# State space projection in another unit order, with the early ada units over fewer steps and a ring of six

## The reference

```python
mod = c_act @ ada_w[i] + ada_b[i]                 # 2048 x 12288, one row vector
sh1, sc1, g1, sh2, sc2, g2 = split(mod, 6)
h = x * (1.0 + sc1) + sh1
u = h @ in_w                                      # 256 x 2048 by 2048 x 2048
lam_bar = exp(lam * dt)
b_bar = ((lam_bar - 1.0) / lam)[..., None] * bmat
bu = einsum('gnp,blgp->lbgn', b_bar, ug)
states = associative_scan(a * s + bu)             # over the tokens, complex
y = real(einsum('gpn,lbgn->blgp', cmat, states)) + d_skip * u
```

## Time and profile before

| | us |
|---|---|
| median of three runs (lowest, highest) | 2490.12 (2487.67, 2490.86) |
| the profiled execution, own time | 2485.89 |
| its span, first to last instruction | 2484.2 |
| TensorE, VectorE, ScalarE busy | 2394.9, 1853.9, 1045.8 |
| state recurrence, from and to | about 218 to 345 |

### The profile page before, as it was taken

The page is one execution under the profiler, slowest core; times in us unless marked ns, Lnnn a source line. Parts: engine busy times, 40 slices in busy tenths (PEclk is TensorE's granted clock), DMA queues, the critical chain, the costliest instruction groups (busy, mean ns, idle before and its releaser), DMA issues.

```text
span 2484.2 us, 33024 instructions
## 1 busy us (share of the span) xinstructions
PE 2394.9 (96%) x12457; PEld 1924.3 (77%) x12457; DVE 1853.9 (75%) x2964; ACT 1045.8 (42%) x1242; POOL 35.3 (1%) x67
## 2 busy tenths in 40 slices
PE   5799799999999999999999999999999999999998
PEld 3377468878888888888878888778888888888886
DVE  6377979977778887889878987887777755455457
ACT  4254024464443444344464444464544344434442
POOL 0000000000000000000000000000000000000000
PEclk9899899999999999999999999999999999999999
DMA  9996938858888998899758877736788666656674
GB/s 308 361 334 229 393 114 291 300 186 295 301 276 300 345 319 271 276 331 313 250 164 301 280 252 231 223 102 195 229 299 294 229 193 188 189 188 199 188 219 144
DMA packets 314686, 627.36 MB, mean 253 GB/s; under 512 B 30656, under 2 KB 31072, under 8 KB 314272
## 3 DMA queue, kind: packets, MB, share of 16 engines
q1 hardware_dynamic: 310240, 611.35, 73.5%
q0 software_dynamic: 4288, 13.90, 2.0%
HBM read 623.05 MB, written 2.10 MB: 252 GB/s over the span
## 4 chain that ended last, share of the span: by engine, by line
PE 85%; DVE 9%; DMA 3%; ACT 2%; issue 1%; SPq 0%; DVEq 0%; ACTq 0%
PE psB L2112 40%; PE psA L2112 39%; DVE prod L1424 2%; DMA col_raw<-in_ada_w 1%; PE psT L1707 1%; DVE tmp L1429 1%; DVE st L1435 1%; PE psM L1739 1%; PE psA L1947 1%; DVE w_lo L1103 1%; DMA Cnat_im<-in_s_c_im 0%; DMA w_raw<-in_dsa_out_w 0%; DVE ada_acc L1120 0%; DVE w_lo_more L1103 0%; DMA w_raw<-in_s_glu_w 0%
## 5 line engine op out<-in xcount | busy, mean ns | idle before, releaser
L1103 DVE TENSOR_TENSOR w_lo<-w_raw,w_hi 128x1024 fp32r<-128x1024 f32 x732 | 893.0, 1223 | 487.0 <-ACT w_hi L784 482.6
L784 ACT ACTIVATE w_hi<-w_raw 128x1024 fp32r<-128x1024 f32 x732 | 774.8, 1060 | 1110.0 <-PE psB L2112 483.6
L2112 PE MATMUL psB<-w_hi,hT_hi 128*128 128x512 f32 x1040 | 407.0, 391 | 0.6 <-DVE w_lo L1103 0.6
L2112 PE MATMUL psB<-w_hi,hT_lo 128*128 128x512 f32 x1040 | 404.9, 389 | 0.0
L2112 PE MATMUL psB<-w_lo,hT_hi 128*128 128x512 f32 x1040 | 404.7, 389 | 0.0
L2112 PE MATMUL psA<-w_hi,hT_hi 128*128 128x512 f32 x1008 | 397.9, 395 | 5.1 <-DVE w_lo L1103 2.0
L2112 PE MATMUL psA<-w_hi,hT_lo 128*128 128x512 f32 x1008 | 393.2, 390 | 0.0
L2112 PE MATMUL psA<-w_lo,hT_hi 128*128 128x512 f32 x1008 | 392.9, 390 | 0.0
L1120 DVE SCALAR_TENSOR_TENSOR ada_acc<-ada_raw,csil,ada_acc 128x512 f32<-128x512 f32 x450 | 336.1, 747 | 13.2 <-DVE ada_acc L1120 0.5
L2112 PEld LDWEIGHTS psB<-w_hi,hT_hi 128*128 128x128 f32 x1040 | 195.2, 188 | 44.7 <-issue 2.8
L2112 PEld LDWEIGHTS psA<-w_hi,hT_hi 128*128 128x128 f32 x1008 | 189.6, 188 | 49.5 <-issue 8.0
(11 more groups left out here) (368 smaller groups left out, 2330.0 us busy)
## 6 DMA issues: line engine op xcount, KB each, us to landing
w_raw<-in_ffn_w_in SPq DMA_DIRECT2D x352, 512.0 KB, 4.6
ada_raw<-in_ada_w SPq DMA_DIRECT2D x480, 256.0 KB, 5.4
w_raw<-in_ffn_w_out SPq DMA_DIRECT2D x176, 512.0 KB, 4.5
col_raw<-in_ada_w SPq DMA_DIRECT2D x128, 512.0 KB, 6.2
w_raw<-in_dsa_in_w SPq DMA_DIRECT2D x112, 512.0 KB, 4.8
w_raw<-in_s_glu_w SPq DMA_DIRECT2D x56, 512.0 KB, 5.7
w_raw<-in_s_in_w SPq DMA_DIRECT2D x32, 512.0 KB, 6.7
w_raw<-in_dsa_out_w SPq DMA_DIRECT2D x32, 512.0 KB, 5.4
```

The source lines that it names most:

```text
L784: nc.scalar.activation(high(u), w_raw[:, u % RING], ACT.Copy).then_inc(w_hi_ready, 1)
L1103: V.tensor_tensor(low(u), w_raw[:, u % RING], high(u).bitcast(F32), ALU.subtract).then_inc(w_lo_ready, 1)
L2112: ins = MM(PS[s][:, t, 0:r.width], a_[:, kt, tok], b_[:, kk, 0:r.width], start=kt == 0 and m == 0, stop=k == r.units - 1 and kk == UK - 1 ...
```

## The change

- `placed` replaces `crossed` and orders all 32 products: first k = 0 to 3 of i = 1, then k = 0 to 3 of i = 0, then k = 4 to 7 of i = 0, and k = 4 to 7 of i = 1 last.
- The half sums of i = 1 are copied from PSUM to `partial` by ScalarE after products 5 and 7; VectorE adds them when i = 1 ends (`finish`), where ScalarE had copied.
- `MIXED` is 40, and 24 columns stand beside products, two for each of twelve.
- The early ada units run from step 16 on (12 steps), in a ring of 6 slots (growA and part of uT, since `partial` has the region more). Slot 4 lies over the staging of h, so unit 4 waits for the last fourth of h (`h_ready`).
- The C table is scaled before BLdiag; `in_pair` and its columns stand before BLdiag is turned.
- `skip_diagonals` is cut in two: 8 tiles at step 30, 8 after the last uT.

```diff
-MIXED = FRONT - AU
+MIXED = FRONT - 24
...
-        early_raw = [at("early_raw0", "growA", [P, 4, AW]), at("early_raw1", "more", [P, 4, AW])]
+        early_raw = [at("early_raw0", "growA", [P, 4, AW]), at("early_raw1", "uT", [P, 2, AW], plus=8 * K)]
+        partial = at("partial", "more", [P, 2, TOK, NB])
...
-        s5_in = Run("u", 2, s5_in_w[0], (0, NB), dense=(0, EARLY, 4, 10), before="x")
+        s5_in = Run("u", 2, s5_in_w[0], (0, NB), dense=(0, EARLY, 4, 16), before="x")
...
-        beside = (4, 4, 4, 2, 2, 0, 0, 0)
-        crossed = [(k, s) for k in range(6) for s in range(2)] + [(6, 0), (7, 0), (6, 1), (7, 1)]
+        beside = (0, 2, 2, 2, 2, 2, 2, 2, 2, 2, 2, 2, 2, 0, 0, 0)
+        closing_early = [(0, 0), (0, 1), (1, 0), (1, 1), (2, 0), (3, 0), (2, 1), (3, 1)]
+        placed = [(1, k, s) for k, s in closing_early]
+        placed += [(0, k, s) for k in range(4) for s in range(2)]
+        placed += [(0, k + 4, s) for k, s in closing_early]
+        placed += [(1, k, s) for s in range(2) for k in range(4, 8)]
...
-                if u >= ARING:
-                    sp.wait_ge(ada_used, u - ARING + 1)
+                ring = 6 if q < EARLY else ARING
+                if u == 4:
+                    sp.wait_ge(h_ready, s5_in.h0 + 4)
+                if u >= ring:
+                    sp.wait_ge(ada_used, u - ring + 1)
...
+                if n >= 2:
+                    for q_, k in ada_units(s5_in, 0, n - 2):
+                        if q_ + k == 0:
+                            sp.wait_ge(col_used, FRONT)
+                        ada_unit(q_, k)
...
+            act.wait_ge(pair_full, 4)
+            act.wait_ge(scaled_ready, 2)
+            h_high(0)
+            hi_unit(0)
             make_h(1)
-            act.wait_ge(pair_full, 4)
-            h_high(0)
             h_high(1)
+            hi_unit(1)
...
+                        if n in (6, 8):
+                            act.wait_ge(w_used, n)
+                            s = (n - 6) // 2
+                            nc.scalar.activation(partial[:, s], PS[s][:], ACT.Copy).then_inc(part_free[s], 1)
...
-            times_lam(pairs(BLdiag[0], True), pairs(BLdiag[1], True), [pairs(b, True) for b in Bdiag], True, scaled_ready)
+            vec.wait_ge(c_stored, 8)
+            times_lam(pairs(Ctab[1][0], False), pairs(Ctab[1][1], False), [pairs(c, False) for c in Ctab[0]], False, c_scaled)
...
+                if r.kind == "u" and i == 1:
+                    vec.wait_ge(w_used, product(r, i, s))
+                    vec.wait_ge(T_full, r.turn + s + 1)
+                    vec.wait_ge(part_free[s], 1)
+                    V.tensor_tensor(stg[s][:], PS[s][:], partial[:, s], ALU.add).then_inc(ps_free[s], 1)
...
+                    if n in (8, 9):
+                        pe.wait_ge(part_free[s], 1)
+                    if i == 1 and k == 4:
+                        pe.wait_ge(ps_free[s], 1)
```

More of the change, by code:

```diff
@@ L560, in product @@
         def product(r, i, s):
-            if r is s5_in and i + s == 0:
-                return r.unit + crossed.index((r.units - 1, 0)) + 1
+            if r is s5_in:
+                return placed.index((i, r.units - 1, s)) + 1
             return r.unit + i * r.per + (s + 1) * r.units
@@ L653, in _ @@
                         elif m == RING:
-                            sp.wait_ge(ada_used, EARLY * AU - ARING // 2)
+                            sp.wait_ge(ada_used, EARLY * AU)
+                        elif m == 6:
+                            sp.wait_ge(T_full, s5_in.turn + 3)
                         col_unit(a)
                     sp.wait_ge(bu_full, 8)
-                for i in range(r.n):
+                for i in range(r.n if r is not s5_in else 0):
                     q = chunk_of(r, i)
@@ L664, in _ @@
                             sp.wait_ge(col_used, glu_after(n - r.units))
-                        elif u >= 8:
+                        else:
                             sp.wait_ge(w_lo_ready, rounded(u - RING))
-                        if u >= 8 and not whole(r, i, n // r.units):
+                        if not whole(r, i, n // r.units):
                             w_unit(r, i, n)
@@ L1845, in _ @@
             for n in range(4, 8):
[L1846 to L1847 removed]
+                turn_diag(n, Bdiag, bdiag_ready, 5, b_stored, b_turned)
+            for n in range(4):
+                in_pair(n)
+                col_units(14 + 2 * n, 16 + 2 * n)
             pe.wait_ge(scaled_ready, 1)
             for n in range(4):
[L1850 to L1851 removed]
+                turn_diag(n, BLdiag, pair_masked, 1, scaled_stored, scaled_turned)
@@ L1882, in crossing @@
                     for t in range(TOK):
-                        ins = products(s5_in, s, k, t, n, hi, lo)
+                        ins = products(r, s, k, t, n, hi, lo, begin, end)
                     ins.then_inc(w_used, 1)
+                    for c in ada_ended(r, 0, n, 2):
+                        sum_chunk(c)
             def inputs(n):
@@ L2155, in _ @@
                     attention()
-                for i in range(r is s5_in, r.n):
+                for i in range(r.n if r is not s5_in else 0):
                     u = r.unit + i * r.per
```

142 lines of the change are left out of this document (72 added, 70 removed).

## The result

| | before | after |
|---|---|---|
| median of four runs each (lowest, highest), us | 2488.89 (2487.51, 2490.86) | 2508.8 (2506.36, 2512.05) |
| profiled execution, own time / span, us | 2485.89 / 2484.2 | 2512.05 / 2510.3 |
| TensorE begins product 0 | 93.7 | 85.1 |
| last front column added (tC) | 126.2 | 144.7 |
| last product of the projection ends | 207.3 | 230.6 |

The changed kernel is slower by about 20 us: the ratio is 1.008, with 1.0063 to 1.0098 as its 95% interval.

What follows compares the result with a forecast made beforehand. Transfers bound the kernel to about 127 us, TensorE from 138 to 207. The new order gains 12 us, the ring returns 16.5 (projection +4.7), 1.6 follow: +6.3 on 2490.1 gives 2496, range 2478 to 2505.

Steps and rivals of the forecast that it cites:

- the ring: Six ada slots in SyncE's in-order queue: two steps take at least a round trip, 8.8 us; gives back 16.5 us.
- what stands behind the last product: Half the skip diagonals on ScalarE after the last uT, 1.4 us, and VectorE adding the last sum, 0.2 us.
- if nothing else bound: Products 16 to 31, three turns and two chunk sums end the projection at 195.5 us, 12 us earlier than before.
- the 212.0 of the sum: Forecast end of the projection's last product with the ring's cost: 212.0 us, against 207.3 before, +4.7 us.
- Up to the last column: Mixed stage, 19.4 MB at 360 GB/s in 53.9 us: last column used at tC = 135.5 us (131 to 140).
- the two moves of partial sums cost nothing: ScalarE's two copies, 1.03 us each, lie beside transfers in the mixed stage and cost nothing.
- The start: Eight columns fewer ahead of unit 0: ScalarE gets it at 80.8 us, product 0 starts near 83.2 (93.7 before).
- hidden by the transfers: Scaling the C table first: its 2 us hide, as what comes next waits for a weight transfer; effect 0.
- From the last column to product 16: ScalarE and VectorE have one more weight unit in between: 12 us, against 10.9 before.
- L: Landing time of a weight unit in the ring's round trip of 4.6 + L; taken as 4.2 us.
- slow transfers: Rival: mixed stage stays at 328 GB/s (+5 us) or L is 5.4 us (+7 us): 2501 to 2508; chance 0.16.
- slack: Rival: the ada ring has slack enough, projection ends at 195.5 us, a gain of 10 us: 2480; chance 0.21.

Runs made afterwards that it cites:

- Experiment 1: The changed kernel with SyncE issuing the ada units of step n - 4, not n - 2, behind weight unit n: 2487.56 us, ratio 1.000.
- experiment 2: The changed kernel with ScalarE's copy of the second partial sum (psB) ahead of the high part of weight unit 10: 2509.47 us, ratio 1.0092.
- experiment 8: The changed kernel with ada units of step n - 4 issued behind weight unit n, and the psB copy placed early: 2487.72 us, ratio 0.9994.
- experiment 9: As experiment 8, but with the tables as in the kernel before (BLdiag scaled first): 2486.54 us, ratio 0.9984.
- experiment 11: As experiment 8, but VectorE leaves out 16 of the 32 additions of the early ada units; all transfers stay: 2486.0 us, ratio 0.9983.
- experiment 12: As experiment 9, but with the early ada units in 13 steps from step 15: 2486.38 us, ratio 0.9985.
- experiment 7: The kernel before with the tables' change alone (C table scaled first, in-pair products and their columns ahead of BLdiag's transposes): 2491.26 us, ratio 1.0011.

## Where the prediction was right and where it was wrong

The direction and the mechanism were right: slower, by the ring of ada units in SyncE's in-order queue. The size was not: 2496 was forecast with 2505 as the upper end, and 2508.8 measured. The sum was made of the ring (+16.5 us), the gain of the new order (-11.8) and what stands behind the last product (+1.6). Experiment 1 takes the ring's cost away and leaves the rest: its ratio of 1.000 (0.999 to 1.0009) says that order and end together are worth 0 and not -10.2 us, and the ring some 20. **So the step that failed most is "if nothing else bound", the 12 us of gain; the second is the ring, 20 us for 16.5.** In the profile the last product ends 18.6 us later than the 212.0 of the sum. By its steps:

- **Up to the last column: 9.2 us.** The sum had tC = 135.5 from the bytes at 360 GB/s, and called TensorE's 3.78 us a step shorter than the transfers' 4.4. A timeline of TensorE shows the column pairs:

```profile
97.68 1.06 PE L1772 MATMUL psM<-col_raw,csil 128*32 128x512 f32 x8
101.63 1.06 PE L1772 MATMUL psM<-col_raw,csil 128*32 128x512 f32 x8
105.57 1.07 PE L1772 MATMUL psM<-col_raw,csil 128*32 128x512 f32 x8
110.29 1.06 PE L1772 MATMUL psM<-col_raw,csil 128*32 128x512 f32 x8 [0.70 <-DMA col_raw<-in_ada_w]
114.89 1.06 PE L1772 MATMUL psM<-col_raw,csil 128*32 128x512 f32 x8 [0.55 <-DMA col_raw<-in_ada_w]
118.83 1.06 PE L1772 MATMUL psM<-col_raw,csil 128*32 128x512 f32 x8
122.95 1.06 PE L1772 MATMUL psM<-col_raw,csil 128*32 128x512 f32 x8
130.54 1.14 PE L1772 MATMUL psM<-col_raw,csil 128*32 128x512 f32 x8
```

  A step without a bracket or gap is 3.94 us: TensorE alone. It also has one product more ahead of the first pair (85.1 + 5.2 + 2.7), three waits for columns of 0.55 to 1.15 us, and a loss of 3.6 us at product 9: 2.1 us of idle time for the copy of psB, then 1.5 us because the product ran at the lower clock (4.49 us). By TensorE's list without waits the end would have been 85.1 + 7.8 for the first two products + 11 x 3.94 + 1.06 = 137.3, and the gap, the waits and a turn of x beside the second pair bring it to 144.7. From product 0 to the last column the sum had 52.3 us. With the copy placed early it is 53.3 to 54.4 us, at 346 to 365 GB/s (experiments 2, 8, 9, 11, 12), 1 to 2 us more than the sum by bytes and the list (52.2) alike. So the rate of 360 was sound, and the term that was wrong in this stage is "the two moves of partial sums cost nothing": in this profile they cost 5 to 6 of the 9.2 us.
- **The start.** Product 0 was forecast at 83.2 and came at 85.1, 1.9 of the 9.2 us. The tables cost 2.7 us by themselves, not 0 (experiment 7): "hidden by the transfers" was wrong because they held up the transfers. With the new tables product 0 begins between 85.1 and 88.9 us in six kernels, with the old ones at 84.7 and 85.1 in two. Two slips of little weight: 80.8 + 53.9 + 1 is 135.7 and not 135.5, and in the kernel before it is the second half of h that 24 products stood behind; behind the last column stood 27.
- **From the last column to product 16:** 13.5 us, forecast 12. It is no term of the 18.6, since the ring sets the end.
- **The ada units.** The round is 4.6 + L, and 9.64 was measured for 8.8. The frame held (the rounds less their landings leave 4.25 to 4.6 us); L was not 4.2 but 6.45 us for weight unit 20 and 5.55, 5.35, 4.65, 4.93 and 6.15 us in the rounds, 5.33 in their mean. Low part 20 was ready at tC + 26.9 (forecast 23.8), 3.1 us late: 2.2 by L and 1.1 because the last fourth of h came late. Low part 30 was ready at tC + 75.1 (67.8), another 4.2 us: 5.6 by L, less 1.4 by the shorter frame. L is thus the largest single error in the profile, 7.9 us. My reason for a small L was that bursts leave on idle queues; but each weight unit leaves right behind ada units. The rival "slow transfers" had this term right with L = 5.4, and its upper end of 2508 is nearest to the result, in part by luck: its 328 GB/s in the mixed stage matches the 324 that was measured, but the late copy had a part in that rate. The Trainium skill, DMA: Bandwidth & Descriptors, "Anatomy of one DMA — SWDGE (gpsimd) path", has the two cost components from which the estimate of 3.2 us for such a transfer alone was worked out; it gives them for transfers that GpSimd issues, and these come from SyncE. No landing in this chain is below 4.65 us, so the trace shows 1.4 to 3.2 us more than that estimate, with ada units issued just ahead of each.
- **"If nothing else bound", 12 us of gain: this was never there.** With the ring's cost taken away the new order is as fast as the old (2487.7, experiment 8), not 12 us faster. Its last product ends at 207.0 and not 195.5: 4.5 us from the later product 0, 2.1 up to the last column, 2.6 from there to product 16, 2.4 behind. Product 0 starts 6 us earlier than before, and TensorE pays for it with four column pairs more beside the products, 1 us each, which it used to do while it waited for transfers. So the price of rival "slack" (2480) would not have come out either: with issue order n - 4 and 24 columns beside products the kernels take 2486 to 2488 us. The part that was right is 48 us for products 16 to 31, which experiment 11 shows as 48.7. Which of the four parts would show in the medians stays open: each is read from one execution.
- **Behind the last product.** ScalarE's second eight diagonals are on the path as said (its timeline):

```profile
233.08 1.02 ACT L941 ACTIVATE uT<-psT 128x1024 f32<-128x1024 f32 x1 [4.18 <-PE psT L1740]
234.00 2.43 ACT L1052 ACTIVATE Ddiag<-ident,dcol 128x128 f32<-128x128 f32 x8
236.34 1.06 ACT L965 ACTIVATE st<-psA 128x512 f32<-128x512 f32 x2
```

  From the last product to glu's first long row 162.65 us pass, 159.68 before: +3.0, forecast +1.6. 1.7 us of it are eight matmuls (L1990) that ran at the lower clock in this one execution (5.34 us, 3.67 before), so +1.3 is the change's.

The sum in the profile: 9.2 + 3.1 + 4.2 + 2.1 (1.7 of it product 30 at the lower clock) = 18.6, and 1.4 behind. These 20 us and the forecast 6.3 give the 26 of the two traces; by the medians the forecast was short by 14, so 6 us of the steps above belong to the two executions that were profiled, and which steps they belong to is not shown.

Of the signs that were named, the pairs of products with gaps, the waits for early_acc (32.0 us) and the diagonals came as said. The last column (144.7, not 131 to 140), the last product's end (230.6, not 205 to 218) and the clock that "stays high" did not: the granted clock was 0.86 from 160 to 231 us.

## What to carry to other kernels

When an edit puts more transfers with slot waits into an in-order queue, work out the round trip (landing, both splits, the additions up to the freed slot, issue) and divide it by the number of steps by which the issue leads the use; compare that with the consumer's step (here the shortest rounds were 4.45 and the mean 4.8 us a step, for a step of 2.72), and mend it by the issue order first, which costs no memory: here n - 4 for n - 2 was worth 21 us. A copy that frees an accumulator is not free if it stands in an in-order list behind work that waits for a transfer. Where two resources are both near full, write down both sums and expect a little more than either (here 53.3 to 54.4 us for 52.2 and 52.3). Work that is moved from a place where its engine waits to a place where it doesn't costs its full time. A step that "hides behind transfers" is free only if it doesn't hold the slots that those transfers need.

## What was not expected of the hardware

Products that came behind idle time ran at the lower of TensorE's two clock levels. In the kernel before, product 0 was the only one of the projection's (4.35 us). In after the engine was busy for 1.06 of the 5 us before, waited 2.82 us for product 0, and was then granted 0.52 of full speed (1.2 of 2.4 GHz) until near 90 us:

```profile
80.00:85.00 5.00, 1.06 (x8) 0.19 (x8) 1.23 (x1) 2.54 (x5) 0.00 (x0) 0.80 1.06 394
85.00:90.00 5.00, 4.90 (x12) 3.94 (x13) 3.50 (x3) 3.32 (x5) 0.00 (x0) 0.52 1.03 402
```

Product 0 took 5.2 us for 2.7, product 9 4.5 us behind 2.1 us of idle time, and product 30, behind a wait of 1.37 us for the last additions, 4.4 us. In the ring the same happened again and again (products 20, 22 and 24 took 4.6 to 5.1 us), which the stretch shows:

```profile
170.00:200.00 30.00, 22.00 (x74) 17.45 (x75) 19.71 (x24) 8.52 (x9) 0.00 (x0) 0.77 0.74 249
```

There no loss can be told, since the chain runs through the transfers and VectorE; it costs only at products 0, 9 and 30, which are on the chain. And a weight unit of 0.524 MB that is issued with two or three ada units took 4.65 to 6.45 us to land while the stretch moved only 244 GB/s; in the kernel before the median of this stage was 6.7 us at 324 GB/s. So a lower mean rate did shorten the landing, but never to the shortest row of 3.7 us; why is not shown.
